# Five cross-partition sums of squares moved from TensorE to GpSimd, and the root that follows them placed later

## What is computed

```python
def rms_norm(x, g):
    xf = x.astype(jnp.float32)
    y = xf * lax.rsqrt(jnp.mean(xf * xf, axis=-1, keepdims=True) + RMS_EPS)
    return (y * g.astype(jnp.float32)).astype(x.dtype)

def shared_kv(x, kv_norm, w_dkv, kv_latent_norm, w_uk, w_uv, cos, sin):
    ckv, k_rope = jnp.split(rms_norm(x, kv_norm) @ w_dkv, [KV_LORA_RANK], axis=-1)
    ckv = rms_norm(ckv, kv_latent_norm)
    k_nope = (ckv @ w_uk).reshape(b, s, MLA_HEADS, QK_NOPE_DIM)
    v = (ckv @ w_uv).reshape(b, s, MLA_HEADS, V_HEAD_DIM)
...
    hn = rms_norm_2(x, norm_ffn_pre[l])
    f = (jax.nn.silu(hn @ w_gate[l]) * (hn @ w_up[l])) @ w_down[l]
```

## Time and profile before

| | |
|---|---|
| median of three runs | 2178.99 us |
| lowest, highest | 2177.45, 2184.60 us |
| span of the profiled execution | 2177.1 us |
| TensorE busy | 2162.9 us, 99% |
| VectorE busy | 1383.4 us, 64% |
| ScalarE busy | 1166.0 us, 54% |
| GpSimd busy | 15.2 us, 1% |
| mean granted TensorE clock | 0.999 of full speed |

### The profile page before, as it was taken

One profiled execution on the slowest core, in us unless ns is written; L12 is line 12 of the kernel. 1 busy time (PEld: TensorE's weight loads), 2 busy tenths in 40 slices (PEclk: granted clock), 3 DMA queues, 4 the chain that ended last, 5 costly groups with the idle time before them and its releaser, 6 DMA issues.

```text
span 2177.1 us, 29335 instructions
## 1 busy us (share of the span) xinstructions
PE 2162.9 (99%) x12058; PEld 1867.9 (86%) x12058; DVE 1383.4 (64%) x1757; ACT 1166.0 (54%) x1543; POOL 15.2 (1%) x30
## 2 busy tenths in 40 slices
PE   9999999999999999999999999999999999999998
PEld 8888888888888888888888888888888888888887
DVE  6565555557787666577657787576656544565655
ACT  6555454655666555566545554565544444444443
POOL 1000000000000000000000000000000000000000
PEclk9999999999999999999999999999999999999999
DMA  7565556455656444565655555556666666666654
GB/s 259 164 182 170 183 164 180 162 192 184 188 166 174 146 147 153 184 200 187 185 183 167 172 167 182 192 160 189 187 192 191 191 194 190 192 189 189 208 184 149
DMA packets 223189, 393.92 MB, mean 181 GB/s; under 512 B 20937, under 2 KB 42962, under 8 KB 222928
## 3 DMA queue, kind: packets, MB, share of 16 engines
q1 hardware_dynamic: 221664, 388.35, 58.0%
q0 software_dynamic: 1248, 3.63, 0.5%
q10 hardware_dynamic: 144, 0.07, 0.0%
HBM read 389.89 MB, written 2.11 MB: 180 GB/s over the span
## 4 chain that ended last, share of the span: by engine, by line
PE 95%; DVE 3%; ACT 1%; issue 0%; DMA 0%; SPq 0%; DVEq 0%; ACTq 0%
PE ps L900 94%; DVE WL L1456 1%; PE ps L910 1%; DVE gT L1459 0%; ACT gT L1181 0%; DVE TMP L1456 0%; DMA XN<-in_x 0%; DVE gT L1456 0%; ACT F L1194 0%; DVE ACC L1456 0%; DVE RAWL L1459 0%; ACT WH L1181 0%; ACT SQ L1181 0%; DVE F L1459 0%; DVE O L1459 0%
## 5 line engine op out<-in xcount | busy, mean ns | idle before, releaser
L1456 DVE TENSOR_TENSOR WL<-RAW,WH 128x1024 fp32r<-128x1024 f32 (+1 forms) x733 | 886.0, 1220 | 436.8 <-ACT WH L1181 434.6
L1181 ACT ACTIVATE WH<-RAW 128x1024 fp32r<-128x1024 f32 (+1 forms) x733 | 767.8, 1055 | 644.1 <-PE ps L900 637.2
L900 PE MATMUL ps<-H,WH 128*128 128x512 f32 x3157 | 1111.0, 397 | 1.2 <-DVE WL L1456 0.6
L900 PE MATMUL ps<-H,WL 128*128 128x256 f32 x3152 | 878.6, 279 | 0.0
L900 PEld LDWEIGHTS ps<-H,WH 128*128 128x128 f32 x3157 | 591.2, 187 | 139.5 <-DVE WL L1456 2.2
L900 PEld LDWEIGHTS ps<-H,WL 128*128 128x128 f32 x3152 | 593.8, 189 | 1.5
L900 PE MATMUL ps<-O,WH 128*128 128x512 f32 (+2 forms) x1383 | 475.2, 391 | 0.2 <-DVE WL L1456 0.2
L900 PE MATMUL ps<-O,WL 128*128 128x256 f32 x1344 | 375.2, 279 | 0.0
L900 PEld LDWEIGHTS ps<-O,WH 128*128 128x128 f32 x1383 | 256.8, 188 | 58.6 <-DVE WL L1456 1.2
L900 PEld LDWEIGHTS ps<-O,WL 128*128 128x128 f32 x1344 | 253.4, 189 | 0.4
L900 PE MATMUL ps<-WH,ACTS 128*128 128x512 f32 x704 | 218.2, 390 | 0.0
(11 more groups left out here) (227 smaller groups left out, 1397.8 us busy)
## 6 DMA issues: line engine op xcount, KB each, us to landing
RAW<-in_w_in_a SPq DMA_DIRECT2D x127, 512.0 KB, 3.7
RAW<-in_w_in SPq DMA_DIRECT2D x96, 512.0 KB, 3.6
RAW<-in_w_gate SPq DMA_DIRECT2D x88, 512.0 KB, 3.7
RAW<-in_w_up SPq DMA_DIRECT2D x88, 512.0 KB, 3.7
RAW<-in_w_down SPq DMA_DIRECT2D x88, 512.0 KB, 3.8
RAW<-in_w_ple_gate SPq DMA_DIRECT2D x64, 512.0 KB, 3.8
RAW<-in_w_in_b SPq DMA_DIRECT2D x40, 512.0 KB, 3.6
RAW<-in_w_out_a SPq DMA_DIRECT2D x32, 512.0 KB, 3.6
```

What stands on the lines that cost most here:

```text
L900: return e.matmul(o, l, r, start=start, stop=True, skip_group_check=True)
L1181: return e.activation(o, i, f, **kw)
L1456: return e.tensor_tensor(o, x, y, op)
```

## The change

The sums over partitions of the five norms `kv`, `ckv`, `cq`, `mixpre` and `ffnpre` are made by one GpSimd instruction each, `partition_all_reduce`, from `ACC[:, 0, :]` to `ACC[:, 1, :]`, which leaves the sum in every partition. It waits for `folded` alone. In the list of steps stands `across` (no engine does anything there), then nine `None` units of `bg`, and then `rstd`, which reads `ACC` in place of a PSUM bank. `ACC` may be written again only when the root is made. The other norms keep their products with ones.

```diff
+ACROSS = ("kv", "ckv", "cq", "mixpre", "ffnpre")
...
+            def rstd_across(norm, pauses):
+                return [do("across", norm), *[None] * pauses, do("rstd", norm, None, makes=[("rs", norm)])]
...
-            pl.bg.append(task(wait_next, None, both(*rstd("kv")), None, None, None, rcols("kv")))
+            pl.bg.append(task(wait_next, None, *rstd_across("kv", 9), None, None, None, rcols("kv")))
...
-                units = [None, None, both(*rstd(name)), None]
+                units = [None, None, *rstd_across(name, 9), None]
...
-            pl.bg.append(task((("next", 1, 3, 1), None), None, None, both(*rstd("mixpre")), None, None, None,
+            pl.bg.append(task((("next", 1, 3, 1), None), None, None, *rstd_across("mixpre", 9), None, None, None,
                               rcols("mixpre")))
...
-            pl.bg.append(task((("h3", KD - 1), None), *[u for q in squares for u in (q, None)], (("fu0",), None), *rstd("ffnpre"),
+            pl.bg.append(task((("h3", KD - 1), None), *[u for q in squares for u in (q, None)], (("fu0",), None), *rstd_across("ffnpre", 9),
                               *scaled, lambda: up(0, 0)))
...
+        def total(norm, b):
+            return ACC[:, 1, :] if norm in ACROSS else ps[:, b, 0:S]
...
-                    act(RW, ps[:, b, 0:S], ACT.Ln, scale=1.0 / NDIM.get(norm, D), bias=EPS[:, :]).then_inc(
+                    act(RW, total(norm, b), ACT.Ln, scale=1.0 / NDIM.get(norm, D), bias=EPS[:, :]).then_inc(
                         *ev(squared, ("ln", norm)))
...
-                    sq_free[0], acc_free[0] = ("rs", norm), ("ones", norm)
+                    sq_free[0], acc_free[0] = ("rs", norm), ("rs" if norm in ACROSS else "ones", norm)
...
-                    dv.wait_ge(at("ln", norm))
-                    ts(RV, ps[:, b, 0:S], 1.0 / NDIM.get(norm, D), ALU.mult, 1e-6, ALU.add).then_inc(
+                    dv.wait_ge(at("ln", norm), at("ones", norm))
+                    ts(RV, total(norm, b), 1.0 / NDIM.get(norm, D), ALU.mult, 1e-6, ALU.add).then_inc(
                         *ev(small, ("var", norm)))
...
+            def across(norm):
+                gp.wait_ge(at("folded", norm))
+                e.partition_all_reduce(ACC[:, 1, :], ACC[:, 0, :], P, bass.bass_isa.ReduceOp.add).then_inc(
+                    *ev(across_done, ("ones", norm)))
...
+            for norm in ACROSS[:3]:
+                across(norm)
             war = next(args[0] for kind, *args in steps if kind == "rtload")
...
+            for norm in ACROSS[3:]:
+                across(norm)
             gp.wait_ge(at("used", plan.h3_read))
```

More of the change, by code:

```diff
@@ L89 @@
     matmul = transpose = activation = tensor_tensor = tensor_scalar = scalar_tensor_tensor = _none
-    memset = tensor_copy = tensor_reduce = reciprocal = dma_start = preload_act_table_set = then_inc = wait_ge = _none
+    memset = tensor_copy = tensor_reduce = reciprocal = dma_start = preload_act_table_set = partition_all_reduce = then_inc = wait_ge = _none
 @dataclass
@@ L360, in build @@
         out_done = sem("out_done")
+        across_done = sem("across_done")
         sig = Signals()
```

## The result

| | before | after |
|---|---|---|
| median | 2178.25 us (4 runs) | 2195.40 us (4 runs) |
| lowest, highest | 2177.45, 2184.60 us | 2193.17, 2198.25 us |
| span of the profiled execution | 2177.1 us | 2191.4 us |
| mean granted TensorE clock | 0.999 | 0.996 |

The ratio of after to before is 1.0070, with a 95% interval of 1.0057 to 1.0083: slower by 0.7%, on the forecast side and inside the range, 5.8 us above the forecast of 2189.6 us. The profiled execution of after is the shortest of its four (2193.17 us); against that of before it is 14.3 us longer. What the other three have more than that comes at the end of the experiments.

A forecast was written before the change was run, and what follows sets the result against it. TensorE, busy 99% of the span, was taken as the bound. Waits of 13.9 us against 3.3 us won gave +10.6 us on 2178.99 us, so 2189.6 us; the range was 2181 to 2214 us.

The forecast's parts named there:

- products gone: Five products with ones leave TensorE: 0.43 us each at `kv`, `mixpre`, `ffnpre`, 0.99 each at `ckv`, `cq`; 3.3 us won.
- wait ahead of `cq`: The late root of `kv` delays evictions and the first low half of `cq`; TensorE waits 4.4 us.
- wait ahead of `kb0`: The late root of `ckv` delays the first low half of `CKV`; TensorE waits 5.4 us.
- `kc0` (root of `mixpre`): The late root of `mixpre` delays the eviction of `qc0`; TensorE waits 1.5 us for a bank in `kc0`.
- `fu1` (root of `ffnpre`): The late root of `ffnpre` delays copying and adding the first pair of `fg1`; TensorE waits 2.6 us.
- wait for the root of `cq`: The root of `cq` lands some 12 us before its product is wanted; no wait, about 3 us to spare.
- length of one sum: One GpSimd sum over partitions taken as 5 us, between 0.42 and 54; shortest cover 11.4 us at `mixpre`, so free.
- lost microsecond for microsecond: Step on TensorE: what leaves it is won, and what makes it wait is lost, at one for one.
- A: Rival: the GpSimd sum outlasts its cover, from 11.4 us on, first at `mixpre`; beyond 2196 us, chance 0.15.
- B: Rival: VectorE's low halves are held up while GpSimd reads; nothing lost at 5 us, 25 us at 10; chance 0.10.
- C: Rival: ScalarE keeps its freed 2.1 us, Ln comes sooner; +5.2 us, 2184.2 us, not slower; chance 0.14.
- D: Rival: the five products go and the roots are hidden, nothing else; 2175.7 us, chance 0.09.

The follow-up runs named there:

- two pauses: Changed kernel with two pauses in place of nine between sum and root at all five norms: 2176.75 us, ratio 0.9987 to the kernel before.
- the kernel with idle products: Changed kernel plus products with unused results ahead of TensorE's three longest waits (18 at `cq`, 22 at `kb0`, 10 in `fu1`): 2193.05 us, ratio 1.0065.
- putting back `kv` alone: Changed kernel with two pauses at `kv` and nine still at the other four norms: 2184.27 us, ratio 1.0025 to the kernel before.
- four sums: Changed kernel with the same GpSimd sum made four times in a row at all five places: 2197.33 us, ratio 1.0079 to the kernel before.
- nine at `ckv` alone: Changed kernel with nine pauses at `ckv` and two at the other four norms: 2175.26 us, ratio 0.9985 to the kernel before.
- `kv` and `ckv` at nine: Changed kernel with nine pauses at `kv` and `ckv`, two at the other three norms: 2188.82 us, ratio 1.0048 to the kernel before.
- two sums more: Two pauses everywhere, with the sums of `pre0` and `conv` on GpSimd as well: 2186.79 us, ratio 1.0037 to the kernel before.

## Why the prediction was right, and where its sum was not

| term | worked out | measured |
|---|---|---|
| products gone | -3.3 | -2.8 (two pauses, ratio; -3.4 by the profiled spans) |
| wait ahead of `cq` (root of `kv`) | 4.4 | 4.1 |
| wait ahead of `kb0` (root of `ckv`) | 5.4 | 5.0 |
| `kc0` (root of `mixpre`) | 1.5 | 1.1 |
| `fu1` (root of `ffnpre`) | 2.6 | 2.4 |
| wait for the root of `cq` | 0 | 0 |
| lower clock behind three waits | none | 5.2 |
| slower pace from 1505 us on | none | 0 in the profiled run, 3.6 to 3.8 where it stood |
| length of one sum | 5 (0.42 to 54) | 2.7 and 1.8, hidden |

**What held.** TensorE is the bound, each microsecond of its waits is lost, and the root lands right ahead of evictions with nothing of the gain left. The four waits came where they were put, each within 0.4 us, and a little short for one common reason: ScalarE reached Ln 0.3 us earlier at `kv` and VectorE passed the root in 2.26 us, not 2.40, since its first step reads `ACC` in 0.29 us where reading PSUM had taken 0.42. At `ckv` the root came 0.6 us later than worked out (648.18 for 647.6), but TensorE wanted it 0.9 us later too (652.8 for 651.9), being at the lower clock behind the wait before.

**What was missed.** The step "lost microsecond for microsecond" lacked what TensorE does behind a wait. The terms end at +10.6 us; the lower clock adds 5.2, and the kernel with idle products shows it: 4.35 us came back by about 1520 us. Together with waits 1.3 us shorter than worked out, that makes +14.5 beside the span's +14.3 us. The median is a further 3 us up, for which the slower pace is a possible and unproven cause. The range held all the same because it was wide enough for both.

**One wait had another origin than its name says.** The prediction read the place of `ckv`'s root off the order and priced it rightly, but did not say whose pauses put it there. They are `kv`'s together with its own: putting back `kv` alone takes away 8.4 us of waits, 3.4 ahead of `cq` and the 5.0 ahead of `kb0`, though `ckv` keeps its nine.

**The rivals.** *A* (a long sum) is out: no Ln waited in after, and even four sums, 8.4 to 11.0 us, cost nothing that can be told from after (1.0079 with an interval that holds 1.0070). The 31 us estimated from the Trainium skill (GPSIMD Engine Reference, Cross-partition — where GPSIMD wins) are eleven times the measured 2.7; that figure is for another instruction. *B* is real in kind, 0.85 us for each sum but that of `ffnpre`, and hidden. *C* (ScalarE keeps its freed time) would bring Ln 2.1 us forward at `kv`; it came 0.3 us sooner, and the `WH` ahead of it waited 0.98 us for TensorE, as the prediction held against C. *D*, that only the products go, does not hold for this change but for the one of two pauses, at 2176.75 us against the 2175.7 worked out.

The best kernels found are those of two pauses (0.9987) and of nine at `ckv` alone (0.9985); their intervals overlap.

## What to carry to other kernels

A delay put into a queue of background work is paid by whatever stands behind it in the queue too: read the place of each later task before and after, and when one delay seems to cost something, put back the one ahead of it first. Give a producer the cover that its latency needs, here two half-chunks for 2.7 us, since more delay only uses up slack at the other end. And where the bounding engine is made to wait for more than a microsecond or two, look at what it does right behind the wait: here that added 5.2 us to 12.6.

## What the runs showed of the hardware

- Behind waits of 4.1 and 5.0 us in after, TensorE ran at its 1.2 GHz level (granted clock 0.50) for some 3 and 4.6 us; behind 4.1 and 5.1 us, with `kv` and `ckv` at nine, for some 5.3 and 6. Behind 2.4 or 2.5 us it did so in three of five profiles for 3 us and in two not at all; behind 2.7 and 3.0 us, with two sums more, for 3.2 and 3.4; behind 1.1 to 1.6 us never.
- A pace 2% under the usual one stood at a granted clock of 1.00, over 200 us in four profiles.
- `partition_all_reduce` of 128x256 float32 takes 2.7 us at `kv`, four in a row 11.0 us, so that the first is not longer than those behind it. It takes 1.8 us where VectorE read PSUM as it began, and single sums of the four lie between these two. The end in the profile is right to 0.03 us.
- Beside each sum of 2.7 us in after, one VectorE instruction with two SBUF inputs was longer: of a pair of `O` the first by 0.85 us, a low half at `cq` and `mixpre` by 0.9 (2.12 us). A low half that had begun 0.2 us ahead of the sum (606.77, 1.22 us) was not, nor one that began 1.2 us into the short sum of `ffnpre` (1490.47, 1.22 us).
